# Query projection of a cross attention: eight block products replaced by seven half-size products and sums on VectorE

## The reference, cut to what matters

```python
h = _layer_norm(DEEPNORM_ALPHA * h + mix, ln1_g[l], ln1_b[l])
xa = _memory_xattn(h, m, w_cq[l], w_ck[l], w_cv[l], w_co[l])
h = _layer_norm(DEEPNORM_ALPHA * h + xa, ln2_g[l], ln2_b[l])
...
def _memory_xattn(h, mem, w_q, w_k, w_v, w_o):
    q = (h @ w_q).reshape(b, s, MEM_HEADS, MEM_HEAD_DIM)      # 768 x 1024 by 1024 x 1024
    k = (mem @ w_k).reshape(b, m, MEM_HEADS, MEM_HEAD_DIM)
    v = (mem @ w_v).reshape(b, m, MEM_HEADS, MEM_HEAD_DIM)
    sc = jnp.einsum('bqhd,bkhd->bhqk', q, k, preferred_element_type=jnp.float32) * (MEM_HEAD_DIM ** -0.5)
    p = jax.nn.softmax(sc, axis=-1).astype(v.dtype)
    o = jnp.einsum('bhqk,bkhd->bqhd', p, v).reshape(b, s, D_MODEL)
    return o @ w_o
```

## Time and profile before

| | |
|---|---|
| median of 3 runs | 1084.79 us (1084.33 to 1085.68) |
| the profiled execution | 1085.32 us |
| its span, first to last instruction | 1083.6 us |
| mean granted TensorE clock | 0.944 of full |
| TensorE busy (matmuls) | 960.0 us, 89% |
| VectorE busy | 416.2 us, 38% |
| GpSimd busy | 295.1 us, 27% |
| ScalarE busy | 234.5 us, 22% |

### The profile page before, as it was taken

The page is one execution under the profiler, slowest core; times in us unless marked ns, Lnnn a source line. Parts: engine busy times, 40 slices in busy tenths (PEclk is TensorE's granted clock), DMA queues, the critical chain, the costliest instruction groups (busy, mean ns, idle before and its releaser), DMA issues.

```text
span 1083.6 us, 10070 instructions
## 1 busy us (share of the span) xinstructions
PE 960.0 (89%) x3432; PEld 502.9 (46%) x3432; DVE 416.2 (38%) x680; ACT 234.5 (22%) x559; POOL 295.1 (27%) x344
## 2 busy tenths in 40 slices
PE   4899999799998899999999999967997999999900
PEld 3466465345444444446657544547343444444300
DVE  5599999954622222000004222244321111112156
ACT  2421133234572021010004301130111111111111
POOL 6721033234444131000005312201152221221137
PEclk9899999899999999999999999975998999999965
DMA  9410303202030003032200150053797999999562
GB/s 330 158 40 0 117 1 103 53 20 59 0 115 2 1 1 125 31 108 86 78 0 1 41 251 39 20 212 115 305 409 305 417 420 420 389 411 394 200 237 116
DMA packets 46230, 166.12 MB, mean 153 GB/s; under 512 B 8514, under 2 KB 13890, under 8 KB 33892
## 3 DMA queue, kind: packets, MB, share of 16 engines
q1 hardware_dynamic: 39460, 152.88, 36.6%
q0 software_dynamic: 6720, 12.60, 3.1%
HBM read 157.92 MB, written 18.03 MB: 162 GB/s over the span
## 4 chain that ended last, share of the span: by engine, by line
PE 58%; DVE 3%; POOL 3%; issue 2%; DMA 2%; ACT 0%; POOLq 0%; SPq 0%; DVEq 0%
PE ps L1601 25%; PE ps L1967 8%; PE ps L1996 7%; PE ps L1970 5%; PE ps L1776 2%; PE ps L1676 2%; PE ps L1944 2%; PE ps L1701 2%; PE ps L1899 1%; POOL hres L647 1%; PE ps L1610 1%; PE ps L1864 1%; DMA hT<-h_rows,gidx 1%; POOL lnc L637 1%; POOL slot_table L855 1%
## 5 line engine op out<-in xcount | busy, mean ns | idle before, releaser
L1601 PE MATMUL ps<-hT,ring 128*128 128x512 f32 (+1 forms) x512 | 167.8, 490 | 1.7 <-ACT hT L903 1.0
L1601 PE MATMUL ps<-ring,hT 128*128 128x512 f32 (+1 forms) x384 | 145.6, 540 | 0.9 <-issue 0.9
L1182 DVE SCALAR_TENSOR_TENSOR cat<-early,cpar,cat 128x798 f32<-128x798 f32 x120 | 131.3, 1094 | 3.8
L1601 PEld LDWEIGHTS ps<-hT,ring 128*128 128x128 f32 x512 | 98.1, 192 | 69.2 <-issue 60.1
L1601 PEld LDWEIGHTS ps<-ring,hT 128*128 128x128 f32 x384 | 72.6, 190 | 71.1 <-issue 68.7
L749 POOL TENSOR_SCALAR hT<-hT,rinv 128x512 f32<-128x512 f32 (+1 forms) x48 | 67.8, 1424 | 97.0 <-DVE rinv L1279 97.0
L815 POOL DMA_INDIRECT pair_rows<-hT,sidx x22 | 22.0, 1001 | 181.1 <-DVE hT L1525 180.3
L1253 DVE TENSOR_REDUCE nmax<-ps 128x1 f32<-128x256 f32 x24 | 10.2, 425 | 154.7 <-PE ps L1676 154.7
L756 POOL TENSOR_SCALAR memx<-memx,rinv 128x256 f32<-128x256 f32 x24 | 22.1, 924 | 154.1 <-DVE rinv L1237 154.1
L1515 DVE COPY memx<-ps 128x256 f32<-128x256 f32 x22 | 9.3, 424 | 131.2 <-PE ps L1979 131.2
L1996 PE MATMUL ps<-ring,memx 128*64 128x512 f32 (+1 forms) x144 | 58.7, 601 | 0.7 <-DVE memx L1515 0.7
(11 more groups left out here) (261 smaller groups left out, 1494.7 us busy)
## 6 DMA issues: line engine op xcount, KB each, us to landing
ring<-w_down SPq DMA_DIRECT2D x16, 1024.0 KB, 16.9
early<-w_gate SPq DMA_DIRECT2D x12, 1024.0 KB, 10.5
early<-w_up SPq DMA_DIRECT2D x12, 1024.0 KB, 14.1
ring<-w_gate SPq DMA_DIRECT2D x10, 1024.0 KB, 13.2
ring<-w_up SPq DMA_DIRECT2D x10, 1024.0 KB, 16.3
scr<-w_down SPq DMA_DIRECT2D x8, 1024.0 KB, 15.7
cat<-w_down SPq DMA_DIRECT2D x8, 1024.0 KB, 15.3
scr<-w_gate SPq DMA_DIRECT2D x5, 1024.0 KB, 10.6
```

The lines of the kernel that those rows point to most:

```text
L1182: ins = v.scalar_tensor_tensor(out=acc[:, c, :], in0=src, scalar=cpar[:, c, k:k + 1], in1=acc[:, c, :], op0=ALU.mult, op1=ALU.add)
L1601: last = t.matmul(out_of(bank), lhs(k), rhs(k), start=(k == 0), stop=(k == KC - 1))
```

## The change

The query projection is a product C = A B with A the turned weights (1024 output columns by 1024) and B the turned tokens (1024 by 768 tokens). Both are cut in half each way: A into A00, A01, A10, A11 of 512 x 512, B into blocks of 512 x 384 tokens. Where the code before forms the eight block products, the new code forms seven (Strassen's scheme in Winograd's form, one level), with these sums:

- of weights: S1 = A10 + A11, S2 = S1 - A00, S3 = A00 - A10, S4 = A01 - S2
- of tokens: T1 = B01 - B00, T3 = B11 - B01, T2 = T3 + B00, T4 = B10 - T2
- products: P1 = A00 B00, P2 = A01 B10, P6 = S2 T2, P7 = S3 T3, P4 = A11 T4, P5 = S1 T1, P3 = S4 B11
- results: C00 = P1 + P2, C01 = P1 + P6 + P5 + P3, C10 = P1 + P6 + P7 + P4, C11 = P1 + P6 + P7 + P5

Each product is made of four column chunks with four contraction chunks each, on 384 token columns. The eight sums S and T are made by VectorE in SBUF, and counted on a new semaphore `combined`. ScalarE copies P1 out of PSUM, VectorE adds the other six to `cat` with the scale. S1 and S2 lie in slot 0 of the ring, S3 and S4 overwrite A10 and A01 in their slots, so `co0` is loaded after P5 and `co1` after P3. The blocks of 384 tokens don't follow the groups of 256 and 512; the attention starts when C00 and C10 are there (P2 and P4) and waits for P3 before its ninth score.

```diff
+CQ_TERMS = ("P1", "P2", "P6", "P7", "P4", "P5", "P3")
+CQ_CHUNKS = KC // 2
+TH = T // 2
...
-    for c in range(KC):
-        for s in range(2):
-            take("mm", ("cq", c, s))
+    for term in CQ_TERMS:
+        for c in range(CQ_CHUNKS):
+            take("mm", ("cq", term, c))
...
+        cq_at = [(slab_names.index(f"cq{j}") % 3) for j in range(2)]
+        cqA = [[ring[:, cq_at[j], 2048 * k:2048 * (k + 1)] for k in range(2)] for j in range(2)]
+        cqS = {"S1": ring[:, 3 - sum(cq_at), 0:2048], "S2": ring[:, 3 - sum(cq_at), 2048:4096],
+               "S3": cqA[1][0], "S4": cqA[0][1]}
+        cqB = [[hTv[:, 4 * k:4 * k + 4, TH * h:TH * (h + 1)] for h in range(2)] for k in range(2)]
...
-                          f"cq{j}": ("cq", 4 * j + 3, 1), f"co{j}": ("co", NT - 1, j)}
+                          f"cq{j}": ("cq", "P3", CQ_CHUNKS - 1), f"co{j}": ("co", NT - 1, j)}
+        slab_last["cv1"] = ("cq", "P5", CQ_CHUNKS - 1)
...
             # ScalarE
-            for c in range(KC):
-                for s, (t0, length) in enumerate(SEQS):
-                    bank = full(act, ("cq", c, s))
-                    a.activation(catv[:, c, t0:t0 + length], bank[:, 0:length], ACT.Copy,
-                                 scale=MHD ** -0.5).then_inc(free(("cq", c, s)), 1)
+            for c in range(CQ_CHUNKS):
+                key = ("cq", "P1", c)
+                bank = full(act, key)
+                a.activation(cq_out(0, 1, c), bank[:, 0:TH], ACT.Copy, scale=MHD ** -0.5).then_inc(free(key), 1)
...
             # VectorE
+            for j in range(2):
+                was_read(dve, ("hT", 1, NT - 1, j))
+            v.tensor_tensor(cqT["T3"], cqB[1][1], cqB[0][1], ALU.subtract).then_inc(combined, 1)
+            dve.wait_ge(combined, 1)
+            v.tensor_tensor(cqT["T2"], cqT["T3"], cqB[0][0], ALU.add).then_inc(combined, 1)
+            slab_wait(dve, "cq0")
+            slab_wait(dve, "cq1")
+            v.tensor_tensor(cqS["S1"], cqA[1][0], cqA[1][1], ALU.add).then_inc(combined, 1)
+            dve.wait_ge(combined, 3)
+            v.tensor_tensor(cqS["S2"], cqS["S1"], cqA[0][0], ALU.subtract).then_inc(combined, 1)
+            v.tensor_tensor(cqS["S3"], cqA[0][0], cqA[1][0], ALU.subtract).then_inc(combined, 1)
+            v.tensor_tensor(cqT["T4"], cqB[1][0], cqT["T2"], ALU.subtract).then_inc(combined, 1)
+            v.tensor_tensor(cqT["T1"], cqB[0][1], cqB[0][0], ALU.subtract).then_inc(combined, 1)
+            dve.wait_ge(combined, 4)
+            def cq_sum(term, out, other, c):
+                return v.scalar_tensor_tensor(out=out, in0=full(dve, ("cq", term, c))[:, 0:TH], scalar=MHD ** -0.5,
+                                              in1=other, op0=ALU.mult, op1=ALU.add)
+            for c in range(CQ_CHUNKS):
+                was_read(dve, ("cq", "P1", c))
+                cq_sum("P2", cq_out(0, 0, c), cq_out(0, 1, c), c).then_inc(free(("cq", "P2", c)), 1)
+            v.tensor_tensor(cqS["S4"], cqA[0][1], cqS["S2"], ALU.subtract).then_inc(combined, 1)
+            for c in range(CQ_CHUNKS):
+                cq_sum("P6", cq_out(0, 1, c), cq_out(0, 1, c), c).then_inc(free(("cq", "P6", c)), 1)
...
+            for c in range(CQ_CHUNKS):
+                was_read(dve, ("cq", "P4", c))
+                cq_sum("P5", cq_out(1, 1, c), cq_out(1, 1, c), c)
+                cq_sum("P5", cq_out(0, 1, c), cq_out(0, 1, c), c).then_inc(free(("cq", "P5", c)), 1)
...
                     # TensorE, scores(u)
+                    if u == SEQS[0][1] // P * MHEADS:
+                        for c in range(CQ_CHUNKS):
+                            was_read(pe, ("cq", "P3", c))
...
             for j in range(2):
-                was_read(pe, ("hT", 1, NT - 1, j))
-            for c in range(KC):
-                w = slab(f"cq{c // 4}")
-                for s, (t0, length) in enumerate(SEQS):
-                    last = product(("cq", c, s), lambda k: k[:, 0:length], lambda k: w[:, k, c % 4 * P:(c % 4 + 1) * P],
-                                   lambda k: hTv[:, k, t0:t0 + length])
-                    done(("cq", c, s), last)
-            for s in range(2):
-                was_read(pe, ("cq", KC - 1, s))
+                was_read(pe, ("hT", 1, MT - 2, j))
+            slab_wait(pe, "cq0")
+            def cq_term(term, w, rows):
+                wk = w.rearrange("p (k c) -> p k c", k=4)
+                for c in range(CQ_CHUNKS):
+                    bank = claim(("cq", term, c))
+                    for k in range(4):
+                        last = t.matmul(bank[:, 0:TH], wk[:, k, c * P:(c + 1) * P], rows[:, k, :],
+                                        start=(k == 0), stop=(k == 3))
+                    done(("cq", term, c), last)
+            cq_term("P1", cqA[0][0], cqB[0][0])
+            cq_term("P2", cqA[0][1], cqB[1][0])
+            pe.wait_ge(combined, 4)
+            cq_term("P6", cqS["S2"], cqT["T2"])
+            pe.wait_ge(combined, 5)
+            cq_term("P7", cqS["S3"], cqT["T3"])
+            pe.wait_ge(combined, 6)
+            cq_term("P4", cqA[1][1], cqT["T4"])
+            pe.wait_ge(combined, 7)
+            cq_term("P5", cqS["S1"], cqT["T1"])
+            pe.wait_ge(combined, 8)
+            cq_term("P3", cqS["S4"], cqB[1][1])
+            for term in ("P2", "P4"):
+                for c in range(CQ_CHUNKS):
+                    was_read(pe, ("cq", term, c))
             attention("x", CROSS, len(SELF))
```

More of the change, by code:

```diff
@@ L293, in encoder, with cq_out @@
         cstd = memx[:, 0:T]
+        cq_at = [(slab_names.index(f"cq{j}") % 3) for j in range(2)]
[3 more added lines that the diff above has]
+        cqB = [[hTv[:, 4 * k:4 * k + 4, TH * h:TH * (h + 1)] for h in range(2)] for k in range(2)]
+        cqT = {"T1": cqB[0][1]}
+        for name, a in (("T2", early[:, 4 * TH:8 * TH]), ("T3", early[:, 0:4 * TH]),
+                        ("T4", scr[:, 2 * T:2 * T + 4 * TH])):
+            cqT[name] = a.rearrange("p (k t) -> p k t", k=4)
+        def cq_out(j, half, c):
+            return catv[:, CQ_CHUNKS * j + c, TH * half:TH * (half + 1)]
         PTP = [hT[:, 2048 * n:2048 * (n + 1)].rearrange("p (h k t) -> p h k t", h=2, k=4) for n in range(2)]
@@ L411, in encoder @@
         u_ready = sem("u_ready")
+        combined = sem("combined")
         qkv_raw, rot_ready = sem("qkv_raw"), sem("rot_ready")
@@ L458, in encoder, with slab_wait @@
             slab_last |= {f"mix{j}": ("mix", NT - 1, j), f"ck{j}": ("ck", 4 * j + 3), f"cv{j}": ("cv", MT - 1, j),
-                          f"cq{j}": ("cq", 4 * j + 3, 1), f"co{j}": ("co", NT - 1, j)}
+                          f"cq{j}": ("cq", "P3", CQ_CHUNKS - 1), f"co{j}": ("co", NT - 1, j)}
+        slab_last["cv1"] = ("cq", "P5", CQ_CHUNKS - 1)
+        def slab_wait(eng, name):
+            n = slab_names.index(name)
+            eng.wait_ge(slab_in[n % 3], 16 * sum(3 if slab_names[m] in ("mix0", "mix1") else 1
+                                                 for m in range(n % 3, n + 1, 3)))
+            return n % 3
         LN_X = list(range(NT))
@@ new lines, in _ @@
+            for c in range(CQ_CHUNKS):
[5 more added lines that the diff above has]
+            for c in range(CQ_CHUNKS):
+                was_read(dve, ("cq", "P6", c))
+                cq_sum("P7", cq_out(1, 1, c), cq_out(0, 1, c), c).then_inc(free(("cq", "P7", c)), 1)
@@ new lines, in _ @@
+            for c in range(CQ_CHUNKS):
+                was_read(dve, ("cq", "P7", c))
+                cq_sum("P4", cq_out(1, 0, c), cq_out(1, 1, c), c).then_inc(free(("cq", "P4", c)), 1)
+            for c in range(CQ_CHUNKS):
[3 more added lines that the diff above has]
+            for c in range(CQ_CHUNKS):
+                was_read(dve, ("cq", "P5", c))
+                cq_sum("P3", cq_out(0, 1, c), cq_out(0, 1, c), c).then_inc(free(("cq", "P3", c)), 1)
@@ L1591, in slab @@
             def slab(name):
[L1592 to L1596, removed]
+                w = w_slabs[slab_names.index(name)][1].shape[1]
+                return ring[:, slab_wait(pe, name), 0:KC * w].rearrange("p (k c) -> p k c", k=KC)
             def product(key, out_of, lhs, rhs):
```

## The result

The changed kernel takes 1070.18 us (median; 1069.66 to 1072.76) against 1085.17 us for the kernel before, beside which it was timed: a ratio of 0.9867, 95% interval 0.9850 to 0.9885; the medians are 15.0 us apart. The profiled execution took 1069.95 us for a span of 1068.2 us. Two further timings of the same kernel gave 0.9879 (0.9862 to 0.9895) and 0.9886 (0.9862 to 0.9910), with medians 13.1 and 10.8 us apart. A ratio is estimated from all executions and need not be the quotient of the medians; the three ratios stand for 14.4, 13.1 and 12.4 us. The forecast was 12.1 us less, 1072.7 us, with a range from 1070.0 to 1075.9 us.

The account below looks back on a forecast made before the run. TensorE alone was taken to bound the query projection; 10.3 us of products plus edges of 0.78 and 0.97 us gave 12.06 us, so 1084.79 us becomes 1072.7 us, own range 1071.3 to 1074.9, widened to 1070.0 to 1075.9 us.

Parts of the forecast that it names:

- The bound: Query projection: TensorE alone sets the stage, VectorE empty beside it; microseconds taken out reach the end one for one.
- The products: Query projection: 224 records of 384 columns at 0.3225 us, 72.25 us against 82.56, saving 10.3 us.
- The rival that prices it as one of 512 columns: Query projection: 384-column matmuls cost 0.4288 us a record, 96.1 us of products, 1096.5 us in all; chance 0.02.
- The edges: Both ends of the query projection: P1 starts 0.78 us earlier, the attention's first score follows without its 0.97 us wait.
- VectorE's prices: Sums in the query projection: 1.77 us a T, 2.31 an S, 0.55 a sum out of PSUM, 31.7 us together.
- The rival on VectorE: Query projection: VectorE's sums pace TensorE, from 2.35 times their prices on; 1075.6 us at three times; chance 0.03.
- Its first step: Before P6: even at twice every price, VectorE's chain takes 16.4 us against 20.6 us of TensorE's P1 and P2.
- Its second step: P5's pair of sums, 2.2 us at twice the price against 2.58; at three times P5 loses about 3 us.
- the forecast's own range: Whole kernel: 1071.3 us (a low run) to 1074.9 us (neither edge won and a high run); chance 0.86.
- the second rival: Stages behind the query projection: gather wait and clock rises move the end up to 3.2 us either way; chance 0.06.
- the rival charged for half clock all through: Query projection: the clock falls; at half clock throughout, 72.25 us become 144.5, 1145 us in all; chance 0.01.
- The loads: Output weights, loaded later, land by 567 us, before their product after the attention: cost nothing, cover 35 us.

Follow-up runs that it names:

- e4: Changed kernel with each of P1's four products made twice, 32 more records of 384 columns: 1083.75 us, ratio 0.9987 to the kernel before.
- e1: The changed kernel timed again with nothing edited: 1072.4 us, ratio 0.9879 to the kernel before.
- e6: Changed kernel with the sums T3, T2, S1 and S2 each made twice on VectorE: 1080.46 us, ratio 0.9952 to the kernel before.
- e7: Changed kernel with T3, T2, S1, S2 made twice and S3, T4, T1 moved behind P2's sums in VectorE's queue: 1076.9 us, ratio 0.9905.
- e8: Changed kernel with each of the 28 sums out of PSUM made three times: 1073.64 us, ratio 0.9894 to the kernel before.
- e3: Kernel before, its eight block products done group by group, with earlier start and earlier attention: 1083.16 us, ratio 0.9982 to the kernel before.
- e10: Changed kernel with three sums doubled on VectorE (T2, S1, S2; T3 made once): 1074.52 us, ratio 0.9909 to the kernel before.
- e5: Kernel before with the loads of the output weights put off as the change does it: 1085.44 us, ratio 0.9995.

## Why the prediction was right

**The bound.** TensorE alone set the stage, and what it lost there reached the end. e4 is the test of that: 32 records put back are 10.33 us in the stage and 11.4 us in the time (1083.75 us, for 1072.4 of e1 beside it), with the spread of what lies behind in the second number.

**The products.** 10.3 us forecast, 82.56 - 72.24 = 10.32 us measured. The record of 384 columns, which no row of before showed, takes 72.24 / 224 = 0.3225 us, the value taken between the neighbours. The rival that prices it as one of 512 columns (0.4288 us) is refuted.

**The edges.** At the start 0.78 us were forecast and 0.95 us measured: P1 starts 0.90 us after the start of the last transposes, against 1.85 us. The forecast took the profile's end of the transposes for the moment at which TensorE is free; P1 starts 0.16 us before that end. At the end 0.97 us forecast, 0.97 us measured (570.47 - 569.50 before, nothing now). The sum is 12.24 us for 12.06.

**VectorE's prices.** 1.77, 2.31 and 0.55 us by the line through the earlier trace rows; 1.76, 2.28 and 0.556 us measured. The total was 31.7 us, the window shows 30.46.

**The rival on VectorE was worked out wrongly,** though its outcome, no pacing, came true. Its first step said that only T3, T2, S1 and S2 stand before P6, with a slack of 11.8 us, and that VectorE could be twice as slow. P6's first product also needs the bank that P2's first sum frees, and that sum stands behind S3, T4 and T1. It ended at 500.32 us, and P6 was due at 505.93: 5.6 us of slack, used up at 1.4 times the prices (14.1 us of work from 486.23 us on). So the forecast was right here with half the room that it named. e6 crossed that point and paid 4.55 us; e7, with another order, did not. Its second step said that P5 would pace TensorE from 2.35 times on and lose 3 us at three times. It compared rates and left out that the debt of four products, some 3 us, fits in the 7.7 us before a bank is claimed again; e8 shows no gap. And the price of a gap was too low: at 2.62 us it brought 1.8 us of half clock with it.

**The surplus and the range.** The measured 1070.18 us lies outside the forecast's own range (1071.3 to 1074.9 us) and only 0.18 us inside the one widened by the second rival, to which the prediction gave a chance of 0.06: that the first timing fell within it has luck in it. The working of the lower ends is loose as well: the lowest run of before is 0.46 us under its median, which gives 1072.2 and not 1071.3 us, and 1070.0 us stands for the rival's 1069.5. The two repetitions, at 1072.4 and 1074.27 us, lie in the own range. 15.0 us against 12.1 is the second rival at its lower side: clock and gather fell well behind the stage. The first trace has a gather of 5.00 us for 8.60 and 2.45 us less behind the first score; the two repetitions came out at 13.1 and 10.8 us. e3 and e4, equal in the stage, differ by 0.6 us in time. That the change has no share at all in what lies behind is not shown to better than about 1 us: the mean of the three timings is 13.0 us by the medians and 13.3 us by the ratios, for 12.2 in the stage.

**The clock.** It stayed at 2.4 GHz (granted 1.00) through 28 short products over four banks. The Trainium skill, TensorE: Matmul & The Clock Gate, section "A second HAM failure mode: psum-queue depth-cycling", puts such a swing down to short idle spells between matmul groups that turn through the PSUM banks. No window of the stage shows a swing, and between the groups TensorE had no such spell: 73.62 of 74.00 us busy. A swing between the levels would also have cost only a part of what the rival charged for half clock all through. Where a spell of 2.62 us was made, in e6, the clock did fall; behind the one of 0.82 us in e10 it did not.

**The loads.** Nothing, as forecast: e5.

## What to carry to other kernels

Price a change of matmul shapes by records and columns: if both fall by an eighth, so does the time, whatever the split between them, as long as TensorE is never kept waiting and its clock stays. Before moving work to an idle engine, list for each wait of the busy one both what it waits for and which buffer it claims, and find where the instruction that frees that buffer stands in the other engine's queue: a matching average load says little, the order decides. Check by the same two moments in each trace what a change does inside its stage, because the rest of this kernel moves by several microseconds from one execution to the next.

## What the runs showed of the hardware

- A gap in TensorE's work of 2.62 us was followed by a granted clock of 0.60 over 4 us, between its levels of 1.2 and 2.4 GHz, and the stage grew by 4.55 us in all; a gap of 0.82 us was followed by 1.00 and the stage grew by 1.07 us. One case of each.
- VectorE at work for 59.09 of 74 us, in SBUF and out of PSUM, left the pace of TensorE's records unchanged: 73.15 us for 73.14.
- One VectorE sum of two SBUF operands and 1024 columns (1.28 us as a rule) took 3.36 us when it started 1.03 us after a sum of GpSimd in SBUF (3.31 us), in e6 and in e7 alike.
- The same program's time from the first score to the end was 510.7, 512.4 and 514.8 us in three executions, and one gather in it took between 5.00 and 8.94 us.
